# Sample states on ScalarE and VectorE, with v rows that travel through memory

## The reference

```python
n1 = _rmsnorm(h, g_mix)
proj = n1 @ w_in                       # 2048 -> 5120: q, f, v, g, u
q = silu(q_raw) * 128 ** -0.5
fg = lb + (1 - lb) * sigmoid(f_raw); k = 1 - fg
# per head (8 heads, 128 x 128 state), for each token:
#   S_t = diag(f_t) S_(t-1) + k_t^T v_t ;  o_t = S_t^T q_t
o = _rmsnorm(o, g_head) * silu(g_raw)
...                                    # multi-scale pooling of u, w_out, FFN, gate
```

## Time and profile before

| | |
|---|---|
| median of 3 runs | 1168.29 us |
| the profiled execution, device time | 1166.37 us |
| its span | 1164.6 us |
| PE busy | 1153.4 us (99%) |
| DVE busy | 1001.7 us (86%) |
| ACT busy | 566.9 us (49%) |
| POOL busy | 73.1 us (6%) |
| moved by DMA | 238.07 MB, 204 GB/s |
| granted PE clock over the span | 0.997 |

### The profile page before, as it was taken

How to read it: one execution, slowest core, us unless ns; L and a number is a source line. 1 busy time by engine, 2 the same in 40 slices (tenths; PEclk the granted TensorE clock), 3 DMA queues, 4 the chain that set the end, 5 groups by cost and what they waited for, 6 DMA issues and landing times.

```text
span 1164.6 us, 30898 instructions
## 1 busy us (share of the span) xinstructions
PE 1153.4 (99%) x12437; PEld 1034.2 (89%) x12437; DVE 1001.7 (86%) x1566; ACT 566.9 (49%) x819; POOL 73.1 (6%) x110
## 2 busy tenths in 40 slices
PE   9999999999999999999999999999999999999997
PEld 7888888888888899899998999989989999999886
DVE  6778799779867898998989989888898999998677
ACT  6545645654555644444444444444444444444544
POOL 2122320101000200000000000000000000000031
PEclk9999999999999999999999999999999999999999
DMA  7767876766566566666666666666666666667595
GB/s 255 240 198 208 237 212 195 233 193 196 182 207 199 181 217 198 196 194 204 216 197 195 193 208 213 194 196 193 213 195 204 215 202 198 204 209 230 175 230 150
DMA packets 199017, 238.07 MB, mean 204 GB/s; under 512 B 12805, under 2 KB 158664, under 8 KB 198672
## 3 DMA queue, kind: packets, MB, share of 16 engines
q1 hardware_dynamic: 192528, 222.13, 61.5%
q0 software_dynamic: 5056, 13.99, 4.2%
q10 hardware_dynamic: 1360, 0.92, 0.3%
HBM read 228.46 MB, written 9.01 MB: 204 GB/s over the span
## 4 chain that ended last, share of the span: by engine, by line
PE 91%; DVE 4%; DMA 2%; issue 1%; ACT 1%; SPq 0%; DVEq 0%; ACTq 0%
PE acc L2343 13%; PE acc L1958 10%; PE acc L1960 10%; PE acc L1962 10%; PE acc L2384 7%; PE acc L2346 6%; PE acc L2345 6%; PE acc L2324 6%; PE acc L2326 6%; PE wrk L2324 4%; PE wrk L2326 4%; PE acc L2387 2%; PE acc L2386 2%; DVE hl L994 2%; PE wrk L2115 1%
## 5 line engine op out<-in xcount | busy, mean ns | idle before, releaser
L994 DVE SCALAR_TENSOR_TENSOR hl<-raw,hl 128x1024 f16<-128x1024 f32 x414 | 493.5, 1219 | 55.4 <-ACT hl L631 52.5
L631 ACT ACTIVATE hl<-raw 128x1024 f16<-128x1024 f32 x414 | 420.7, 1052 | 166.9 <-DMA raw<-in_w_down_dram 91.7
L2343 PE MATMUL acc<-nrm,hl 128*128 128x264 f16 x1344 | 274.8, 276 | 0.0
L1960 PE MATMUL acc<-nrm,hl 128*128 128x264 f16 x920 | 253.9, 276 | 0.0
L1962 PE MATMUL acc<-nrm,hl 128*128 128x264 f16 x920 | 253.9, 276 | 0.0
L1958 PE MATMUL acc<-nrm,hl 128*128 128x264 f16 x920 | 253.9, 276 | 0.0
L2345 PE MATMUL acc<-nrm,hl 128*128 128x264 f16 x672 | 185.5, 276 | 0.0
L2346 PE MATMUL acc<-nrm,hl 128*128 128x264 f16 x672 | 185.5, 276 | 0.0
L2343 PEld LDWEIGHTS acc<-nrm,hl 128*128 128x128 f16 x1344 | 129.0, 98 | 17.8 <-DVE tg L1502 0.2
L2384 PE MATMUL acc<-big,hl 128*128 128x264 f16 x704 | 130.2, 276 | 0.0
L1958 PEld LDWEIGHTS acc<-nrm,hl 128*128 128x128 f16 x920 | 90.2, 98 | 13.3 <-issue 0.3
(11 more groups left out here) (491 smaller groups left out, 2246.7 us busy)
## 6 DMA issues: line engine op xcount, KB each, us to landing
raw<-in_w_gate_up_dram SPq DMA_DIRECT2D x168, 512.0 KB, 4.6
raw<-in_w_down_dram SPq DMA_DIRECT2D x88, 512.0 KB, 4.0
raw<-in_w_in_dram SPq DMA_DIRECT2D x80, 512.0 KB, 4.5
raw<-in_w_out_dram SPq DMA_DIRECT2D x32, 512.0 KB, 5.2
raw<-in_w_ple_gate_dram SPq DMA_DIRECT2D x32, 512.0 KB, 5.3
state<-in_state_hgrn_dram POOLq DMA_DIRECT2D x8, 512.0 KB, 6.9
out_new_hgrn_sample_dram<-state POOLq DMA_DIRECT2D x8, 512.0 KB, 5.2
raw<-in_w_gate_up_dram SPq DMA_DIRECT2D x16, 256.0 KB, 3.7
```

Of the source, the lines that this page charges most:

```text
L631: nc.scalar.activation(hi[:, st.hl_slot(j, half), :], raw[:, st.raw_slot(j), :], ACT.Copy, scale=WSCALE).then_inc(hi_done, 1)
L994: stt(lo[:, st.hl_slot(j, half), :], raw[:, st.raw_slot(j), :], WSCALE, hi[:, st.hl_slot(j, half), :], ALU.mult, ALU.subtract).then_inc(lo ...
L1960: mm(out, wh, x_lo[:, kt, :], start=False, stop=False)
L2343: mm(out, wh, n_hi[:, kt, :], start=jj == 0 and kk == 0, stop=False, skip_group_check=bool(up))
```

## The change

The outer products and the transposes that feed them leave PE. DVE packs v of a quad's samples (`vs_pack`, 128 x 32), PE transposes it once (job `vs`), ACT copies the 32 x 128 result out (`value_rows`), POOL stores it to a scratch tensor in memory (`v_rows`) and reads it back so that all 128 partitions hold the 8 rows of one head (`rows_to_all`, 512 KB written for each head, 4 MB in all). ACT then multiplies, with the column of f or k as its scale, each of the 8 old states of a head and each of the 8 rows (`sample_part`, 4 instructions of 128 x 128 each, 16 for a head: 128 in all). DVE adds the two 128 x 1024 tiles (`new_states`, 8 in all). The halves of the states follow later (`S_HI_AT`), and the job `os` stands at 42, 52, 65 and 72 (before 36, 48, 60 and 68). The sum of squares moves from step 71 to 74, its root from 72 to 75, `sample_mix` from 75 to 77. The window buffers are zeroed after the last store of a state.

```diff
-SAMPLE_AT = (26, 38, 50, 58)
-BUF_AT, U_LAST_AT, OSS_AT = 44, (73, 80), 71
-RMS_AT, ROOT_AT, SAMPLE_ROOT_AT = 64, 65, 72
-O_NORM_AT, O_MIX_AT, SAMPLE_MIX_AT = (66, 67, 69, 71), (68, 70, 72, 74), 75
+PART_AT = ((28, 29, 30, 31, 32, 33, 34, 35), (40, 41, 42, 43, 44, 44, 45, 46),
+           (50, 51, 54, 54, 56, 56, 57, 58), (59, 60, 63, 64, 64, 65, 66, 66))
+ADD_AT = tuple((at[3] + 1, at[7] + 1) for at in PART_AT)
+S_HI_AT = ((36, 38), (46, 48), (59, 61), (67, 68))
+S_OUT_AT = (42, 52, 65, 72)
+ROWS_AT = (26, 51)
+BUF_AT, U_LAST_AT, OSS_AT = 44, (73, 80), 74
+RMS_AT, ROOT_AT, SAMPLE_ROOT_AT = 64, 65, 75
+O_NORM_AT, O_MIX_AT, SAMPLE_MIX_AT = (66, 67, 69, 71), (68, 70, 72, 74), 77
...
-X_FIRST = 27
+X_ROWS, X_FIRST, X_LAST = 16, 24, 28
...
-            nc.gpsimd.memset(scores[:, 0:2], 0.0)
-            nc.gpsimd.memset(kv_wide[0], 0.0)
-            for n in range(2):
-                last = nc.gpsimd.memset(win[n][:, :, 0:WPAD], 0.0)
-            last.then_inc(zero_ready, 1)
+            nc.gpsimd.memset(scores[:, 0:2], 0.0).then_inc(zero_ready, 1)
...
-            x_blocks(range(BUF_BEHIND, X_FIRST))
+            def rows_written(c):
+                pool.wait_ge(drained["act"], drain_of(f"vs_{c}")[1])
+                pool.dma_start(v_rows[c], vs_tok).then_inc(vs_out, 16)
+            def rows_to_all(h):
+                n = NSAMP * P
+                src = bass.AP(v_rows.tensor, v_rows.offset + h * n, [[0, P], [1, n]])
+                pool.dma_start(v_bc[h % 2].rearrange("p b v -> p (b v)"), src).then_inc(v_bc_in[h % 2], 16)
+            x_blocks(range(BUF_BEHIND, X_ROWS))
+            rows_written(0)
+            x_blocks(range(X_ROWS, X_ROWS + 2))
+            pool.wait_ge(vs_out, 16)
+            rows_to_all(0)
+            rows_to_all(1)
+            x_blocks(range(X_ROWS + 2, X_FIRST))
...
+                if p == 2:
+                    rows_written(1)
+                    pool.wait_ge(vs_out, 32)
+                    rows_to_all(4)
+                    rows_to_all(5)
...
-                    pool.wait_ge(drained["dve"], drain_of(f"ou_{p}_3")[1])
+                    pool.wait_ge(state_new, h + 1)
...
+                    if p % 2 == 0:
+                        rows_to_all(h + 2)
+                    if h == 0:
+                        x_blocks(range(X_FIRST, X_LAST))
...
-                    x_blocks(range(X_FIRST, 4 * (SEQ // 32)))
+                    x_blocks(range(X_LAST, 4 * (SEQ // 32)))
...
-                    pool.wait_ge(job_done, job_value("sb"))
-                    nc.gpsimd.memset(kv_wide[1], 0.0).then_inc(zero_ready, 1)
...
+            for n in range(2):
+                last = nc.gpsimd.memset(win[n][:, :, 0:WPAD], 0.0)
+            last.then_inc(zero_ready, 1)
...
-            def sample_part(p, r):
-                if r == 0:
-                    wait_job(f"kv_{p}")
-                    if p:
-                        wait_job(f"ou_{p - 1}_3")
-                    nc.scalar.activation(kv_smp, wrk[:, JOB[f"kv_{p}"] % JOB_BANKS, :].bitcast(F16)
-                                         .rearrange("p (s h j d) -> p s h j d", s=2, h=2, j=2), ACT.Copy)\
-                        .then_inc(drained["act"], 1)
-                elif r in (5, 6):
-                    h = 2 * p + r - 5
-                    act.wait_ge(drained["dve"], drain_of(f"ou_{p}_3")[1])
-                    if p:
-                        wait_job(f"os_{p - 1}")
-                    nc.scalar.activation(s_hi[h % 2], state[:, h % 2], ACT.Copy).then_inc(s_hi_ready, 1)
+            def value_rows(c):
+                wait_job(f"vs_{c}")
+                nc.scalar.activation(vs_tok, wrk[0:4 * NSAMP, JOB[f"vs_{c}"] % JOB_BANKS, 0:P], ACT.Copy)\
+                    .then_inc(drained["act"], 1)
+            def sample_part(p, n):
+                old, h = n % 4 // 2 == p % 2, 2 * p + n // 4
+                x, gains = (state[:, h % 2], f_all) if old else (v_bc[h % 2], k_all)
+                if old:
+                    act.wait_ge(state_in[h % 2], 16 * (p + 1))
+                    act.wait_ge(acc_free, TPG * (3 * (p // 2) + 3))
+                else:
+                    act.wait_ge(v_bc_in[h % 2], 16 * (p + 1))
+                for b in range(4 * (n % 2), 4 * (n % 2) + 4):
+                    last = nc.scalar.activation(x[:, b, :], x[:, b, :], ACT.Copy, scale=gains[:, h, SEQ + b:SEQ + b + 1])
+                if n % 2:
+                    last.then_inc(state_kept if old else kv_ready, 1)
+            def state_high(h):
+                act.wait_ge(state_new, h + 1)
+                if h > 1:
+                    wait_job(f"os_{h // 2 - 1}")
+                nc.scalar.activation(s_hi[h % 2], state[:, h % 2], ACT.Copy).then_inc(s_hi_ready, 1)
...
+                if b in ROWS_AT:
+                    value_rows(ROWS_AT.index(b))
...
-                    sample_part(p, b - SAMPLE_AT[p])
+                    for n in range(8):
+                        if PART_AT[p][n] == b:
+                            sample_part(p, n)
+                    if b in S_HI_AT[p]:
+                        state_high(2 * p + S_HI_AT[p].index(b))
...
-            def pair_states(p, bs):
-                for h in range(2):
-                    dve.wait_ge(state_in[h], 16 * (p + 1))
-                for bb in bs:
-                    name = f"ou_{p}_{bb}"
-                    wait_job(name)
-                    for n in range(4):
-                        h, b = n // 2, 4 * (n % 2) + bb
-                        s = state[:, h, b, :]
-                        last = stt(s, s, f_all[:, 2 * p + h, SEQ + b:SEQ + b + 1], bank(name)[:, n * P:(n + 1) * P],
-                                   ALU.mult, ALU.add)
-                    drain(last, name)
+            def new_states(h):
+                dve.wait_ge(state_kept, h + 1)
+                dve.wait_ge(kv_ready, h + 1)
+                tt(state[:, h % 2], state[:, h % 2], v_bc[h % 2], ALU.add).then_inc(state_new, 1)
...
-                hs, wide = slice(4 * c, 4 * c + 4), kv_wide[c]
+                hs = slice(4 * c, 4 * c + 4)
...
-                dve.wait_ge(zero_ready, c + 1)
+                nc.vector.tensor_copy(vs_pack.rearrange("p (h b) -> p h b", h=4), v_all[:, hs, SEQ:TOK]).then_inc(vs_packed, 1)
...
-                src = [x[:, hs, SEQ:TOK].unsqueeze(3).to_broadcast([P, 4, NSAMP, 2]) for x in (k_all, v_all)]
-                wide = [wide[:, n].rearrange("p (h b) r -> p h b r", h=4) for n in range(2)]
-                nc.vector.tensor_copy(wide[0][:, :, :, 0:2], src[0])
-                link(nc.vector.tensor_copy(wide[1][:, :, :, 0:4:2], src[1]))
-                tt(wide[0][:, :, :, 2:4], src[0], wide[0][:, :, :, 0:2], ALU.subtract)
-                tt(wide[1][:, :, :, 1:4:2], src[1], wide[1][:, :, :, 0:4:2], ALU.subtract).then_inc(kv4_ready, 1)
...
-            def sample_rest(p, r):
-                if r in (2, 4):
-                    pair_states(p, (r - 2, r - 1))
-                elif r in (6, 7):
-                    h = 2 * p + r - 6
+            def sample_rest(p, b):
+                if b in ADD_AT[p]:
+                    new_states(2 * p + ADD_AT[p].index(b))
+                if b - 1 in S_HI_AT[p]:
+                    h = 2 * p + S_HI_AT[p].index(b - 1)
...
-                elif r == 10:
+                if b == S_OUT_AT[p]:
...
-                if b == SAMPLE_AT[-1] + 10:
+                if b == S_OUT_AT[-1]:
...
-            def sample_kv(p):
-                pe.wait_ge(kv4_ready, p // 2 + 1)
-                out = job(f"kv_{p}").bitcast(F16)
-                for n in range(8):
-                    at = 16 * (p % 2) + 4 * (n % 4)
-                    last = nc.tensor.transpose(out[:, n * P:(n + 1) * P],
-                                               kv_wide[p // 2][:, n // 4, at:at + 4, :].rearrange("p c r -> p (c r)"),
-                                               ident16[:])
-                    if n == 7:
-                        last.then_inc(job_done, 1)
-                    yield
+            def sample_values(c):
+                pe.wait_ge(vs_packed, c + 1)
+                out = job(f"vs_{c}")
+                nc.tensor.transpose(out[0:4 * NSAMP, 0:P], vs_pack, ident[:]).then_inc(job_done, 1)
+                yield
...
-            def outer(p, bs):
-                if bs[0] == 0:
-                    pe.wait_ge(drained["act"], drain_of(f"kv_{p}")[1])
-                for bb in bs:
-                    out = job(f"ou_{p}_{bb}")
-                    rows = slice(32 * bb, 32 * bb + 4)
-                    for n in range(4):
-                        last = mm(out[:, n * P:(n + 1) * P], kv_smp[rows, 0, n // 2, n % 2, :],
-                                  kv_smp[rows, 1, n // 2, n % 2, :], start=True, stop=True)
-                    last.then_inc(job_done, 1)
...
+                if b in ROWS_AT:
+                    yield from sample_values(ROWS_AT.index(b))
...
-                    yield from sample_jobs(p, b - SAMPLE_AT[p])
+                    yield from sample_jobs(p, b)
...
```

33 lines of the change are left out of this document (14 added, 19 removed).

## The result

The changed kernel takes 1175.02 us, the median of four runs (1173.46 to 1176.28), against 1168.03 us of the kernel before on the same chip: ratio 1.0065, 95% interval 1.0051 to 1.0079, so it is slower, by some 0.65%. I had predicted 1170.7. The range held the time, but I had forecast 2.4 us more and it is 7.0.

A forecast was written before the change was run, and what follows sets the result against it. PE, 99% busy, was taken to set the time: -5.1 + 0.9 + 2.6 + 3.4 + 0.9 - 0.3 = +2.4 us on the median 1168.29, so 1170.7; range 1165.0 to 1175.5.

The forecast's parts named there:

- the clock: PE's granted clock, 0.997 over the span, was taken to stay at the 2.4 GHz level, with no cost.
- the price of a multiplication: On ACT, a 128 x 128 multiplication with a column as scale: 0.20 us, 0.8 for four; bounds 0.17 and 0.27.
- PE's own work: Transposes (1.8 us) and outer products (3.5) leave PE, two float32 transposes (0.2) come: -5.1 us.
- Block 51: PE stops for keys that ACT packs behind DVE's later level: +0.9 us, bounds 0 and 1.6.
- Block 56: PE stops because ACT's parts of step 54 wait for v rows, round trip 10 us: +2.6, bounds 0.3 and 8.8.
- Rival (d): On ACT, multiplications with a column don't overlap, 0.28 us apart; blocks 72 +1.3, 56 +0.6: 1172.6 us; chance 0.10.
- Block 72: PE waits for ACT's eviction of u, behind `mix_high` and DVE's second `mix_part`: +3.4 us, bounds 2.4 and 4.4.
- Block 80: PE stops for `sample_mix`, now behind two splits and a window, 4.5 us later: +0.9, range 0.4 to 1.5.
- The sum: Whole kernel: PE's own work, four stops and the 0.3 us stop gone at block 84 make +2.4 us.

The follow-up runs named there:

- the kernel with a number: Changed kernel with all multiplications by 0.5 instead of by a column of f or k, so scaling is wrong; 1172.74 us, ratio 1.0045 to the kernel before.
- a quarter of the multiplications: Changed kernel with 96 of the 128 multiplications left out, all waits, additions, halves and transfers kept; ratio 1.0005 to the kernel before.
- DVE's part: Changed kernel with additions and low halves of the last two heads covering one sample instead of eight; 1170.95 us, ratio 1.0030 to the kernel before.
- both stops filled: Changed kernel with 34 matmuls filling PE's stop ahead of block 56 and 34 ahead of block 72; 1173.26 us, ratio 1.0055 to the kernel before.

## Why the prediction was wrong

Three steps failed: the clock, which was put at nothing (2.6 us); the path from ACT's multiplications over the root to PE in block 68, which was left out (1.8 us); and the price of a multiplication, 0.20 us instead of 0.29, which rests on a misreading of a row of the kernel before. Term by term:

- **PE's own work, -5.1 us:** right, 5.1 by the blocks without stops.
- **Block 51, +0.9:** 1.0, and 0.3 more two blocks on. Right.
- **Block 56, +2.6:** the place, the cause and the 187.8 us of the copy were right; it was 3.9. Of the 1.3 us, the trip was 10.6 instead of 10 (rows at 198.74, not 197.8: 0.9 with the start of the store), the eight multiplications 2.35 instead of 1.6 (0.75), the gates 0.2 more, less 0.5, since PE wanted the block 0.5 later than I had it. The trip isn't steady: with an earlier store it took 13.0 us (184.52 to 197.48).
- **A multiplication, 0.20 us:** this step failed. I compared the three instructions with a column with a group of four with a number that took 1.46 us, took these to be back to back, 0.36 apart, and so found 0.10 for the column in all three together. They are not back to back: the fourth waited for PE's last matmul of block 71. The trace of the kernel before, in two windows:

```profile
251.88 0.94 ACT L722 ACTIVATE big<-acc 128x264 f32<-128x264 f32 x3
...
252.94 0.39 ACT L722 ACTIVATE big<-acc 128x264 f32<-128x264 f32 x1
```

  The first three take 0.94 us and end at 252.82, the fourth starts at 252.94. So those three are (0.94 - 0.39) / 2 = 0.27 apart, and three with a column take 1.21: 0.27 more, or 0.09 for each, which is what the kernel with a number measured. So this trace agrees with the 93 ns of the Trainium skill ("ScalarE: Activation LUTs", section "What ACT_TABLE_LOAD costs"), where the prediction says that it doesn't. With the pair at 0.17 this gives 0.26. The 0.03 left is not the column's, since with a number these multiplications are 0.20 apart; the pair at 0.17 reads accumulators and doesn't write in place, and which of these differences makes the 0.03 no run told. Rival (d), to which I gave 0.10, had the price nearly right (0.28) by the wrong mechanism: it had the instructions not overlap at all, but they last 0.39 and overlap by 0.10. The price made block 68's stop (1.8; with a number 0.3 is left), which the prediction doesn't have at all: I followed ACT's list to the eviction and never to the root and PE's transposes of the normalised outputs.
- **Block 72, +3.4:** 3.9. The mechanism, one addition and two low halves on DVE behind a longer list on ACT, was shown from both sides. That the size came out so near is partly luck: counted from block 64, the eviction of u starts 28.5 us behind it instead of 22.6, so 5.9 later and not 3.7, and the column's price on 24 multiplications makes 2.2 of it by the kernel with a number; but PE came 1.8 later than I had it, by the stop at block 68, and that hid most of the difference.
- **Block 80, +0.9:** none, because PE came later than I had it. It was hidden: in three kernels in which the stop at 72 was cut by 2.5 us or more or lost its slow matmuls (a quarter of the multiplications, DVE's part, both stops filled) 0.9 to 1.0 us came at block 80; where that stop fell only to 3.2 (a number in place of the column), none did.
- **The clock:** this step failed too, and is the largest missing term, 2.6 us. I had written that I take the clock to stay at 2.4 GHz; it fell behind both stops of 3.9 us, and didn't where they were filled.
- **The sum:** +2.4 had to be +2.4 + 1.3 (56) + 1.8 (68) + 0.5 (72) - 0.9 (80) + 2.6 (clock) + 0.3 = +8.0, against 7.9 in the traces from block 26 to 84; the medians differ by 7.0. So most of the excess lies in what the stops trigger and in a stop that I didn't look for, and not in the four places that I had priced.

## What to carry to other kernels

Where an engine is busy all the time and others work in strict lists beside it, work taken off it is worth what the lists' least slack allows; add up each list not only to the wait that you expect, but to every instruction on it that someone waits for. A stop is dearer than its length once the matmul clock falls behind it (1.3 to 2.9 us more in these traces), and a stop mended at one place often shows the next one's slack, so judge a table of steps by the sum of stops over the whole stage. Take the price of an instruction from a row of its own shape and its own operands, or measure it before 128 of them are placed; and before a group of rows is divided by its count, look whether its last one waited for something.
